# The down projection of both gated MLPs by seven block products per pair of output tiles

## The chip, the cores and the metric

The kernel runs on one NeuronCore of one Trainium2 chip. The metric is the device time of one execution in microseconds (us). All matrix work is float32, carried out as sums of three float32r products.

## What is computed

A trunk of two residual layers over 512 tokens of width 1024 and a final RMSNorm. Layer 0 mixes tokens by an S5 group and an mLSTM group, layer 1 by sliding-window attention. Each layer ends with the gated MLP that this change is about:

```python
def conv_gated_mlp(xn, w_up, conv_w, conv_b, w_down):
    gate, val = jnp.split(xn @ w_up, 2, axis=-1)
    return (jax.nn.silu(causal_dwconv(gate, conv_w, conv_b)) * val) @ w_down

h = h + conv_gated_mlp(rmsnorm(h, norm_ffn_g[layer]), ffn_w_up[layer], ffn_conv_w[layer],
                       ffn_conv_b[layer], ffn_w_down[layer])
```

`w_up` is 1024 x 5632, `w_down` is 2816 x 1024. The hidden width 2816 is 22 blocks of 128.

## The kernel before

Everything is held transposed: features on the 128 partitions, the 512 tokens along the free axis. `h` is the residual stream (8 blocks). A float32 product is made exact enough by splitting both operands into a float32r high part and the rest: `whi` and `wlo` for a weight tile, `ahi` and `alo` for an activation. `block3` then issues three matmuls per 128 x 128 block (high x high, high x low, low x high), each over 512 tokens. ScalarE (ACT) makes the high parts with a copy, VectorE (DVE) the low parts with a subtraction (`split_hi`, `split_lo`); weight tiles (512 KB) come by DMA into two buffers of `raw` and go on to a ring of four in `whi` and `wlo`. The load of a tile waits until `split_lo` of the tile two ahead of it is done.

**Up projection.** The first 4 of the 22 hidden blocks (`PLAIN`) go that way. The other 18 go in pairs, a gate tile with its value tile, by the seven-product form of a 2 x 2 block product: class `Pair`, 18 per layer. The activations are cut in quarters (4 blocks x 256 tokens): `b11`, `b21`, `b22` and the differences `t1` to `t4`. The weights of a pair are cut in quarters too and combined. GpSimd (POOL) makes the sums s1 and s3 in `fold` and three low parts (`pair_s1`, `pair_s3`, `pair_gate_lo`, `pair_keep_lo`, `pair_s3_lo`), DVE makes s2 and s4 in PSUM and three low parts (`pair_s2`, `pair_s2_lo`, `pair_s4`, `pair_s1_lo`, `pair_s4_lo`), ACT the high parts. TensorE (PE) then runs seven products P1, P2, P6, P5, P7, P3, P4 in that order, `quarter`, each 12 matmuls over 256 tokens, and DVE adds them up in `pair_u2`, `pair_u4` and `pair_row`. Convolution and gate (`pair_tap`, `pair_conv`, `pair_silu`, `pair_gated`) follow and write block j of the activation `a32`. The quarters of the activations are made once per layer, before pair 0: `turned_x` on POOL (the differences), `x_high` on ACT, `x_low` on DVE.

**Down projection.** For each of the 8 output tiles m, three weight tiles (8, 7 and 7 blocks) and 22 calls of `block3`. The four PSUM banks 0 to 3 take turns, so that a tile may start while three others wait to be added to `h`:

```python
            def down(i, m):
                pe.wait_ge(out_freed, i * 4 + (O_DN[l] + m - 3))
                for part, ks in enumerate(parts):
                    t = T_DN[l] + 3 * m + part
                    pe.wait_ge(lo_done, i * 12 + (t + 1))
                    for k in ks:
                        if k in ready:
                            pe.wait_ge(*ready[k])
                        ins = block3(bank[(O_DN[l] + m) % 4][:, :], t % RING, k - ks[0], ahi[:, k, :],
                                     alo[:, k, :], k == 0, k == FJ - 1)
```

The first tile takes each block k as it becomes ready, the last ones (`a_low`) while it already runs. Each engine works its list in the order in which it is written; semaphores with counts tie the lists together. An instruction that waits holds up all behind it on its engine.

Of the kernel before, what the change touches and what calls it, by code (L numbers as in the profile page):

```python
# [48 lines left out]
T_UP = [27, 77]  # L49
T_DN = [T_UP[0] + 2 * PLAIN, T_UP[1] + 2 * PLAIN]  # L50
T_QKV = T_DN[0] + 3 * KB
NQKV = 10
T_WO = T_QKV + NQKV
T_END = T_DN[1] + 3 * KB
# [11 lines left out]
NPAIR = FJ - PLAIN  # L66
# [4 lines left out]
A_GROUPS = ((2, 6), (6, 10), (10, 14), (14, 18), (18, 20), (20, 21), (21, 22))  # L71
A_POOL = ((2, 4),)
A_DVE = ((4, 6), (6, 8), (8, 10), (10, 12), (12, 14), (14, 16), (16, 18), (18, 20), (20, 21), (21, 22))
X_HI = {"b11": 1, "b21": 2, "t1": 3, "t3": 4, "t2": 5, "b22": 7, "t4": 8}
A_FIRST_HI, HI_EACH, LO_EACH, TURNED_EACH = 6, 8 + len(A_GROUPS), 7 + len(A_DVE), 5 + len(A_POOL)


def a_group(j):
    return 9 + [k for k, (j0, j1) in enumerate(A_GROUPS) if j0 <= j < j1][0]
# [41 lines left out]
class Pair:  # L121
# [12 lines left out]
    def block(self):  # L134
        return PLAIN + self.c

# [36 lines left out]
def build(nc, wstream, spairs, xT, params, bc, consts, band, outT, u_scratch):  # L173
# [78 lines left out]
    alo_at = base + size([P, FJ, SEQ]) + 4 * LINE  # L252
    assert past_a + 2112 + 2 * 2048 + 1024 <= alo_at
    alo = at("alo", [P, FJ, SEQ], alo_at, f32r)
    a32 = at("a32", [P, FJ, SEQ], alo_at)
    raw2 = at("raw2", [P, 2, 8 * P], alo_at + size([P, FJ, SEQ]))
# [154 lines left out]
    p1_kept, keep_high, keep_low = half_in[0:3]  # L411
# [3 lines left out]
    rstd_bank = bank[6]  # L415

# [6 lines left out]
    last_bank = (bank[(O_DN[1] + KB - 1) % 4], bank[4])  # L423
# [16 lines left out]
    def _(sp):  # L440
# [71 lines left out]
        def pair_loads(l):  # L512
# [20 lines left out]
        loads(T_DN[0] + 1, T_QKV + 5)  # L533
        sp.wait_ge(tile_used, used_count(T_DN[0] + 3 * KB - 1))
# [18 lines left out]
    def _(pool):  # L553
# [2123 lines left out]
```

## Time and profile before

| what | value |
|---|---|
| median of 3 runs | 1029.65 us (1029.28 to 1033.05) |
| the profiled execution | 1028.86 us, its span 1027.3 us |
| TensorE busy | 1012.5 us, 99% of the span |
| VectorE, ScalarE, GpSimd busy | 68%, 53%, 48% |
| up pairs, layer 0 and layer 1 | about 256 to 426 us and 728 to 897 us |
| down projection, layer 0 and layer 1 | about 426 to 547 us and 897 to 1019 us |

The span is cut in stages that follow each other. A share over the whole says little: in the stretch of the up pairs DVE and POOL are near 80% busy, in that of the down projection under 50% and 10%.

### The profile page before, as it was taken

How to read it: one execution, taken by the hardware profiler on the slowest of the kernel's cores; microseconds unless marked ns; L12 is line 12 of the kernel's file. 1: busy time of each engine (PE TensorE's matmuls, PEld its weight loads, DVE VectorE, ACT ScalarE, POOL GpSimd, SP SyncE). 2: the span in 40 equal slices, each digit the busy share in tenths (PEclk: the TensorE clock that was granted, in tenths of full speed). 3: DMA queues.
4: the chain of work that ended last, by engine and by line, in shares of the span. 5: the costliest groups of instructions: out<-in, count | busy, mean ns of one | idle time of the engine just before them, and what ended most of it. 6: DMA issues, size and time to landing. Idle time of an engine off the chain costs nothing.

```text
span 1027.3 us, 18159 instructions
## 1 busy us (share of the span) xinstructions
PE 1012.5 (99%) x6848; PEld 886.4 (86%) x6848; DVE 700.5 (68%) x1020; ACT 541.0 (53%) x939; POOL 489.4 (48%) x437
## 2 busy tenths in 40 slices
PE   9999999999999999999999999999999999999997
PEld 8787778887999999978888777888999999978886
DVE  6798774499877787853334776568987787873332
ACT  6545674456665666732323565464666666732221
POOL 8998930454878777200110122244877877501100
PEclk9999999999999999999999999999999999999999
DMA  7442024221333232243224111242223223133322
GB/s 240 164 122 53 26 96 173 94 103 62 124 123 123 87 118 82 82 144 123 102 100 156 51 54 63 66 140 83 94 112 123 108 97 123 61 125 121 103 82 82
DMA packets 31293, 107.47 MB, mean 105 GB/s; under 512 B 7232, under 2 KB 9536, under 8 KB 26368
## 3 DMA queue, kind: packets, MB, share of 16 engines
q1 hardware_dynamic: 31232, 106.69, 30.5%
q8 instruction: 34, 0.56, 0.2%
q14 instruction: 27, 0.22, 0.1%
HBM read 102.09 MB, written 3.15 MB: 102 GB/s over the span
## 4 chain that ended last, share of the span: by engine, by line
PE 81%; DVE 11%; issue 2%; ACT 2%; DMA 2%; SPq 1%; POOL 0%; DVEq 0%; ACTq 0%
PE bank L2054 15%; PE bank L2056 14%; PE bank L2055 14%; PE bank L2364 11%; PE bank L2363 11%; PE bank L2365 11%; DVE wlo L1379 2%; PE bank L2078 2%; DVE alo L1731 2%; DMA raw<-wstream 1%; DVE t_lo L1731 1%; PE bank L2503 1%; PE bank L2480 1%; DVE b_lo L1731 1%; DVE a L1801 1%
## 5 line engine op out<-in xcount | busy, mean ns | idle before, releaser
L1379 DVE TENSOR_TENSOR wlo<-raw,whi 128x1024 fp32r<-128x1024 f32 x105 | 143.7, 1373 | 104.2 <-ACT whi L877 103.7
L877 ACT ACTIVATE whi<-raw 128x1024 fp32r<-128x1024 f32 x105 | 110.7, 1055 | 141.5 <-PE bank L2056 87.4
L2363 PE MATMUL bank<-t_hi,shi 128*128 128x256 f32 x576 | 159.9, 278 | 3.6 <-DVE bank L1737 3.6
L2365 PE MATMUL bank<-t_hi,slo 128*128 128x256 f32 x576 | 159.7, 277 | 0.0
L2364 PE MATMUL bank<-t_lo,shi 128*128 128x256 f32 x576 | 159.7, 277 | 0.0
L2054 PE MATMUL bank<-xhi,whi 128*128 128x512 f32 x384 | 151.9, 396 | 0.8 <-DVE wlo L1379 0.8
L2055 PE MATMUL bank<-xlo,whi 128*128 128x512 f32 x384 | 149.6, 390 | 0.0
L2056 PE MATMUL bank<-xhi,wlo 128*128 128x512 f32 x384 | 149.6, 390 | 0.0
L2054 PE MATMUL bank<-ahi,whi 128*128 128x512 f32 (+1 forms) x374 | 141.5, 378 | 0.5 <-DVE alo L1731 0.3
L2056 PE MATMUL bank<-ahi,wlo 128*128 128x512 f32 (+1 forms) x374 | 140.9, 377 | 0.0
L2055 PE MATMUL bank<-alo,whi 128*128 128x512 f32 (+1 forms) x374 | 140.9, 377 | 0.0
L583 POOL TENSOR_TENSOR ssum<-ssum,sq 128x512 f32<-128x512 f32 x27 | 39.5, 1464 | 201.1 <-ACT sq L883 201.1
L802 POOL TENSOR_TENSOR slo<-raw,shi 128x1024 fp32r<-128x1024 f32 x36 | 88.8, 2468 | 82.0 <-ACT shi L1179 82.0
L2363 PE MATMUL bank<-b_hi,shi 128*128 128x256 f32 x432 | 119.5, 277 | 0.0
L2364 PE MATMUL bank<-b_lo,shi 128*128 128x256 f32 x432 | 119.3, 276 | 0.0
L2365 PE MATMUL bank<-b_hi,slo 128*128 128x256 f32 x432 | 119.3, 276 | 0.0
L2363 PEld LDWEIGHTS bank<-t_hi,shi 128*128 128x128 f32 x576 | 108.7, 189 | 4.0 <-DVE bank L1737 4.0
L2365 PEld LDWEIGHTS bank<-t_hi,slo 128*128 128x128 f32 x576 | 108.9, 189 | 0.0
L2364 PEld LDWEIGHTS bank<-t_lo,shi 128*128 128x128 f32 x576 | 108.8, 189 | 0.0
L2054 PEld LDWEIGHTS bank<-xhi,whi 128*128 128x128 f32 x384 | 72.1, 188 | 17.6 <-DVE wlo L1379 1.2
L2056 PEld LDWEIGHTS bank<-xhi,wlo 128*128 128x128 f32 x384 | 72.1, 188 | 15.2
L2055 PEld LDWEIGHTS bank<-xlo,whi 128*128 128x128 f32 x384 | 72.1, 188 | 14.6 <-issue 0.2
(309 smaller groups left out, 2240.3 us busy)
## 6 DMA issues: line engine op xcount, KB each, us to landing
raw<-wstream SPq DMA_DIRECT2D x105, 512.0 KB, 3.3
raw<-spairs SPq DMA_DIRECT2D x36, 1024.0 KB, 4.8
xin<-xT SPq DMA_DIRECT2D x8, 256.0 KB, 6.3
raw<-wstream SPq DMA_DIRECT2D x8, 256.0 KB, 5.4
h<-xT SPq DMA_DIRECT2D x1, 2048.0 KB, 8.1
u_scratch<-uperm SPq DMA_DIRECT2D x1, 1024.0 KB, 5.4
uc<-u_scratch SPq DMA_DIRECT2D x8, 128.0 KB, 4.4
bandsb<-band SPq DMA_DIRECT2D x1, 1024.0 KB, 4.8
```

The costliest lines, as they stand in the source:

```text
L583: G.tensor_tensor(ssum[:, :], ssum[:, :], sq[:, m % 2, :], ALU.add).then_inc(acc_done, 1)
L802: G.tensor_tensor(slo[:, two, :], raws[p.par][:, 0, :].rearrange("p (b f) -> p b f", b=2), shi[:, two, :].bitcast(f32), ALU.subtract).then ...
L877: A(whi[:, t % RING, :], raw[:, t % RAWS, :], ACT.Copy).then_inc(hi_done, 1)
L1379: V.tensor_tensor(wlo[:, t % RING, :], raw[:, t % RAWS, :], whi[:, t % RING, :].bitcast(f32), ALU.subtract).then_inc(lo_done, 1)
L1731: V.tensor_tensor(dst, src, hi.bitcast(f32), ALU.subtract).then_inc(sem, 1)
L2054: MM(dst, wh, rhi, start=start, stop=False)
L2055: MM(dst, wh, rlo, start=False, stop=False)
L2056: return MM(dst, wl, rhi, start=False, stop=stop)
L2078: return nc.tensor.transpose(dst, src, ident[0:k, 0:k])
L2363: MM(dst, wh, hi[:, b, :], start=b == 0, stop=False)
L2364: MM(dst, wh, lo[:, b, :], start=False, stop=False)
L2365: ins = MM(dst, wl, hi[:, b, :], start=False, stop=b == 3)
```

## The change

Of the 22 blocks of the down projection, 0 to 5 (`KEPT`) stay plain: one weight tile of 6 blocks for each m, and two PSUM banks in turn (1 and 3) in place of four. Blocks 6 to 13 and 14 to 21 are two chunks. In each chunk the eight output tiles go as four pairs (m, m+1) through the same class `Pair` and the same engines' routines, so that a layer has 26 pairs: 18 up and 8 down, numbered 0 to 25 here. The quarters of the activations are now made three times per layer, for the up pairs and for each chunk, from `a32`. Each down pair ends with an addition of two rows of `h` (`pair_added`, two operands in SBUF, 128 x 1024), each plain tile with one (`kept_added`, one operand in PSUM, 128 x 512). The core of the diff (lines left out at "..."):

```diff
-NPAIR = FJ - PLAIN
+NUP = FJ - PLAIN
+CHUNKS, KEPT = 2, 6
+NPAIR = NUP + CHUNKS * KB // 2
...
+    def kept_bank(m):
+        return bank[(1, 3)[m % 2]][:, :]
...
             for q in range(2, NPAIR):
...
+                if q == NUP + 1:
+                    pair_used(Pair(l, NUP - 1))
+                    for t in range(T_DN[l], T_DN[l] + KB):
+                        load(t, t % RAWS, t - 1)
+                    sp.wait_ge(lo_done, T_DN[l] + KB)
+                else:
+                    pair_used(Pair(l, q - 2))
                 sp.dma_start(raws[q % 2][:, :, :], spairs[NPAIR * l + q]).then_inc(pair_in[q % 2], 16)
...
             pair_tap(last.before())
             pair_p1(last)
             a_high(l, 2, 6)
             pair_silu(last.before())
             act.wait_ge(product_done, last.count(7, P2))
-            split_hi(d0)
-            a_high(l, 6, 10)
...
+            split_hi(d0, w=KEPT * P)
+            x_high(l, "b11", product_done, last.count(7, P2), 0)
             act.wait_ge(product_done, last.count(7, P5))
+            split_hi(d0 + 1, w=KEPT * P)
             act.wait_ge(product_done, last.count(7, P3))
+            split_hi(d0 + 2, w=KEPT * P)
+            x_high(l, "b21", product_done, last.count(7, P3), 0)
             pair_tap(last)
+            split_hi(d0 + 3, w=KEPT * P)
             pair_silu(last)
...
+            x_high(l, "t4", xt_made, made + 9, 0)
+            split_hi(d0 + 6, w=KEPT * P)
+            pair_s1_copy(p)
+            split_hi(d0 + 7, w=KEPT * P)
+            pair_gate_hi(p)
...
+        def kept_added(l, m):
+            wait_tile_used(dve, T_DN[l] + m)
+            V.tensor_tensor(h[:, m, :], h[:, m, :], kept_bank(m), ALU.add).then_inc(out_freed, 1)
+
+        def pair_added(p):
+            m, made = p.rows(), parts_of(p)
...
+            both = drow_pair[:, :, 0:2 * QW]
+            V.tensor_tensor(h[:, m:m + 2, :], h[:, m:m + 2, :], both, ALU.add).then_inc(down_added, 1)
...
+            for q in range(NUP + 1, LAST):
+                p = Pair(l, q)
+                pair_row(p.before())
+                pair_added(p.before())
+                pair_s4_lo(p)
+                pair_s2(p.after())
+                pair_u2(p)
+                finished(p.before())
+                pair_s2_lo(p.after())
+                pair_s4(p.after())
+                pair_s1_lo(p.after())
+                if p.chunk() == 0:
+                    x_low(l, next(names), 1)
+                pair_u4(p)
+                if p.chunk() == 0:
+                    x_low(l, next(names), 1)
+                    if q == NUP + 3:
+                        x_low(l, next(names), 1)
...
+            finished(p.before())
+            split_lo(T_QKV)
+            pair_u4(p)
+            split_lo(T_QKV + 1)
+            split_lo(T_QKV + 2)
+            pair_row(p)
+            pair_added(p)
+            finished(p)
...
+            for m in range(KB):
+                t = T_DN[l] + m
+                pe.wait_ge(lo_done, t + 1)
+                if m == 1:
+                    pe.wait_ge(a_done, FJ * (l + 1))
+                if m >= 2:
+                    pe.wait_ge(out_freed, O_DN[l] + m - 1)
+                for k in range(KEPT):
...
+                    ins = block3(kept_bank(m), t % RING, k, ahi[:, k, :], alo[:, k, :], k == 0, k == KEPT - 1)
+                ins.then_inc(tile_used, 1)
+            for q in range(NUP, LAST):
+                pair(Pair(l, q))
```

`finished` makes, for the pairs of chunk 1, two low parts of the next layer's input (`xlo`, layer 0) or two rows of the output (`outb`, layer 1). The last pair of layer 1 runs its products as P1, P6, P5, P7, P3, P2, P4, so that the second half of the tokens is complete before the last two products. The sums of squares of `h` (`add_square`) for rows 0 to 3 move among the last two pairs on POOL.

How the lists change at the place where the plain tiles run, layer 0. First DVE before, from the sum `pair_u2` of the last up pair on (`wlo` is `split_lo` of a down tile, `alo` is `a_low`; `u4u` and the `rows` behind it are the last pair's sums, `bank<-rows,prm,bank` its convolution, `a<-rows,bank` its gate):

```order
L1768 TENSOR_TENSOR rows<-bank,p_68 128x2x256
L1801 TENSOR_TENSOR a_70<-rows,bank 128x512
L1379 TENSOR_TENSOR wlo<-raw,whi 128x1024
L1731 TENSOR_TENSOR alo<-a_70,ahi 128x1024 x2
L1773 TENSOR_TENSOR u4u_89<-bank,rows 128x512
L1776 TENSOR_TENSOR rows<-bank,u4u_89 128x256
L1731 TENSOR_TENSOR alo<-a_70,ahi 128x1024
L1379 TENSOR_TENSOR wlo<-raw,whi 128x1024
L1731 TENSOR_TENSOR alo<-a_70,ahi 128x1024
L1781 TENSOR_TENSOR rows<-bank,u4u_89 128x2x256
```

The same engine of the changed kernel, from the gate of the last up pair to the addition of the third plain tile (`h<-h,bank` is `kept_added`; `alo<-a,h_b` and `l_t<-f_t,h_t` are `x_low` of chunk 0):

```order
L1990 TENSOR_TENSOR a_70<-rows,bank 128x512
L1541 TENSOR_TENSOR wlo<-raw,whi 128x768
L1959 TENSOR_TENSOR h<-h,bank 128x512
L1541 TENSOR_TENSOR wlo<-raw,whi 128x768
L1893 TENSOR_TENSOR alo<-a_70,h_b_102 128x4x256
L1893 TENSOR_TENSOR alo<-a_70,h_b_103 128x4x256
L1959 TENSOR_TENSOR h<-h,bank 128x512
L1893 TENSOR_TENSOR l_t_105<-f_t_98,h_t_104 128x1024
L1541 TENSOR_TENSOR wlo<-raw,whi 128x768
L1893 TENSOR_TENSOR l_t_107<-f_t_100,h_t_106 128x1024
L1959 TENSOR_TENSOR h<-h,bank 128x512
```

What moved: six `alo` operations are gone, seven `x_low` have come, and the additions that free a bank for PE now stand behind two or three operations that read both operands from SBUF.

POOL of the changed kernel at the same place (before, one `alo` subtraction of 128 x 1024 and then only the sums of squares stand here). The `f0` rows are the differences of chunk 0, the `f1` rows those of chunk 1, `fold` and `slo` the weights of pairs 18 (`raw2`) and 19 (`raw`):

```order
L879 TENSOR_TENSOR f0_t1_98<-a32_70 128x1024
L879 TENSOR_TENSOR f0_t3_100<-a32_70 128x1024
L879 TENSOR_TENSOR f0_t2_99<-a32_70,f0_t1_98 128x1024
L879 TENSOR_TENSOR f0_t4_101<-a32_70,f0_t2_99 128x1024
L852 TENSOR_TENSOR fold_67<-raw2_72 128x512
L858 TENSOR_TENSOR fold_67<-raw2_72 128x512
L879 TENSOR_TENSOR f1_t1_112<-a32_70 128x1024
L879 TENSOR_TENSOR f1_t3_114<-a32_70 128x1024
L879 TENSOR_TENSOR f1_t2_113<-a32_70,f1_t1_112 128x1024
L864 TENSOR_TENSOR slo_74<-raw2_72,shi_73 128x1024
```

POOL, idle in this stretch before, has ten operations in a row, all SBUF to SBUF.

DVE of the changed kernel in the period of one down pair of chunk 0 (pair 20, with `h<-h,drow` the addition of pair 19):

```order
L1970 TENSOR_TENSOR h<-h,drow 128x1024
L1893 TENSOR_TENSOR slo<-bank,shi 128x512
L1899 TENSOR_TENSOR bank<-bank,raw 128x512
L1937 TENSOR_TENSOR drow<-bank,p_68 128x2x256
L1893 TENSOR_TENSOR slo<-bank,shi 128x512
L1907 TENSOR_TENSOR bank<-raw,bank 128x512
L1893 TENSOR_TENSOR slo<-bank,shi 128x512
L1893 TENSOR_TENSOR l_t_119<-f_t_112,h_t_118 128x1024
L1943 TENSOR_TENSOR du4u_92<-bank,drow 128x512
L1949 TENSOR_TENSOR drow<-bank,du4u_92 128x256
L1893 TENSOR_TENSOR l_t_121<-f_t_114,h_t_120 128x1024
L1955 TENSOR_TENSOR drow<-bank,du4u_92 128x2x256
```

Against an up pair, convolution and gate (three operations with one operand in PSUM) are gone; `h<-h,drow` and two `x_low`, with both operands in SBUF, have come.

## Rows read from the trace of the kernel before

**Rows 1.** The page, part 1: TensorE's busy time, share of the span, instructions.

```profile
PE 1012.5 (99%) x6848; PEld 886.4 (86%) x6848; DVE 700.5 (68%) x1020; ACT 541.0 (53%) x939; POOL 489.4 (48%) x437
```

**Rows 2.** Windows: busy us and instructions per engine, granted clock, DMA share, GB/s.

```profile
256.00:420.00 164.00, 162.81 (x1422) 162.84 (x1423) 131.19 (x207) 103.03 (x172) 126.37 (x84) 0.99 0.31 109
440.00:560.00 120.00, 120.00 (x530) 99.06 (x529) 49.91 (x53) 39.36 (x46) 9.69 (x8) 1.00 0.36 120
```

**Rows 3.** Timeline of PE, plain tiles and up pairs: start, duration, operation.

```profile
300.06 0.28 PE L2363 MATMUL bank<-b_hi,shi 128*128 128x256 f32 x1
...
301.08 0.28 PE L2363 MATMUL bank<-t_hi,shi 128*128 128x256 f32 x1
...
559.73 0.39 PE L2054 MATMUL bank<-xhi,whi 128*128 128x512 f32 x1
...
563.58 0.39 PE L2056 MATMUL bank<-xhi,wlo 128*128 128x512 f32 x1
```

**Rows 4.** Timeline of DVE and of POOL, 225 to 234 us.

```profile
225.84 1.42 DVE L1379 TENSOR_TENSOR wlo<-raw,whi 128x1024 fp32r<-128x1024 f32 x1
227.18 3.41 DVE L1379 TENSOR_TENSOR wlo<-raw,whi 128x1024 fp32r<-128x1024 f32 x1
230.51 3.43 DVE L1731 TENSOR_TENSOR b_lo<-xn,b_hi 128x1024 fp32r<-128x1024 f32 x1
...
226.13 3.38 POOL L817 TENSOR_TENSOR f_t<-xn,f_t 128x1024 f32<-128x1024 f32 x1
229.59 3.27 POOL L817 TENSOR_TENSOR f_t<-xn,f_t 128x1024 f32<-128x1024 f32 x1
```

**Rows 5.** Timeline of DVE and of POOL where the down tiles' splits begin.

```profile
422.16 1.92 DVE L1379 TENSOR_TENSOR wlo<-raw,whi 128x1024 fp32r<-128x1024 f32 x1
424.01 1.21 DVE L1731 TENSOR_TENSOR alo<-a,ahi 128x1024 fp32r<-128x1024 f32 x1
...
420.58 2.42 POOL L821 TENSOR_TENSOR alo<-a,ahi 128x1024 fp32r<-128x1024 f32 x1 [4.36 <-ACT ahi L1215]
```

**Rows 6.** Timeline of DVE and of POOL in the period of one up pair.

```profile
393.01 0.68 DVE L1801 TENSOR_TENSOR a<-rows,bank 128x512 f32<-128x512 f32 x1
...
392.24 2.42 POOL L802 TENSOR_TENSOR slo<-raw,shi 128x1024 fp32r<-128x1024 f32 x1 [2.06 <-ACT shi L1179]
394.62 1.30 POOL L807 TENSOR_TENSOR slo<-raw,shi 128x512 fp32r<-128x512 f32 x1
```

**Rows 7.** Timeline of DVE, the last up pair's work, and of ACT.

```profile
420.96 0.69 DVE L1768 TENSOR_TENSOR rows<-bank,p 128x512 f32<-128x512 f32 x1 [0.99 <-PE bank L2365]
...
426.28 0.68 DVE L1773 TENSOR_TENSOR u4u<-bank,rows 128x512 f32<-128x512 f32 x1
...
428.46 1.22 DVE L1379 TENSOR_TENSOR wlo<-raw,whi 128x1024 fp32r<-128x1024 f32 x1
...
433.60 0.75 DVE L1790 SCALAR_TENSOR_TENSOR bank<-rows,prm,bank 128x512 f32<-128x512 f32 x1
...
433.19 1.06 ACT L877 ACTIVATE whi<-raw 128x1024 fp32r<-128x1024 f32 x1 [0.95 <-DMA raw<-wstream]
```

**Rows 8.** Windows and timeline of PE: two waits of PE before early pairs.

```profile
258.00:260.00 2.00, 2.00 (x13) 2.00 (x12) 2.00 (x4) 1.60 (x3) 2.00 (x2) 0.58 0.31 49
...
257.19 0.36 PE L2363 MATMUL bank<-t_hi,shi 128*128 128x256 f32 x1 [2.37 <-DVE bank L1737]
```

**Rows 9.** Timeline of ACT and DVE at the end of layer 0.

```profile
550.09 0.61 ACT L901 ACTIVATE sum_hi<-ssum 128x512 fp32r<-128x512 f32 x1
...
549.40 1.14 DVE L1911 SCALAR_TENSOR_TENSOR xlo<-h,prm,xhi  x1 [1.62 <-ACT xhi L1309]
...
551.60 0.68 DVE L1392 TENSOR_TENSOR sum_lo<-ssum,sum_hi 128x512 fp32r<-128x512 f32 x1
```

**Rows 10.** Timeline of DVE at the kernel's end.

```profile
1018.91 0.42 DVE L2020 TENSOR_TENSOR h<-h,bank 128x256 f32<-128x256 f32 x1 [2.78 <-PE bank L2056]
...
1021.93 2.22 DVE L2025 TENSOR_TENSOR outb<-outb,rstd 128x256 f32<-128x256 f32 x4
```

More of the change, by code:

```diff
@@ new lines, in chunk_high, with next_high @@
+            def chunk_high(name):
+                if name == "t4":
+                    act.wait_ge(product_done, Pair(l, NUP + 3).count(7, P1))
+                if name == "b22":
+                    act.wait_ge(xt_made, made + 11)
+                need = {"b11": 13, "b21": 13, "t1": 10, "t3": 11, "t2": 12, "b22": 12, "t4": 13}[name]
+                x_high(l, name, xt_made, made + need, 1)
+            m_last = KB if l == 0 else KB - 2
+            n = 2 + 2 * l
+            def next_high(p):
+                act.wait_ge(down_added, p.added())
+                for m in (p.rows(), p.rows() + 1):
+                    A(xhi[:, m, :], h[:, m, :], ACT.Copy, scale=col("g_mix1", m)).then_inc(xhi_done, 1)
@@ L1817, in mlp @@
             g = "g_ffn%d" % l
-            first, last = Pair(l, 0), Pair(l, NPAIR - 1)
+            first, last = Pair(l, 0), Pair(l, NUP - 1)
             plain = [Pair(l, k - PLAIN) for k in range(PLAIN)]
@@ L1867, in mlp @@
             pair_u4(first)
-            for q in range(1, NPAIR - 1):
+            for q in range(1, NUP - 1):
                 period(Pair(l, q))
+            p = last.after()
             pair_row(last.before())
@@ L1918, in mlp @@
[L1918 to L1928 removed]
+            split_lo(d0 + 3, w=KEPT * P)
@@ new lines, in mlp @@
+            kept_added(l, 0)
+            split_lo(d0 + 4, w=KEPT * P)
+            x_low(l, "b11", 0)
+            x_low(l, "b21", 0)
+            kept_added(l, 1)
+            x_low(l, "t1", 0)
+            split_lo(d0 + 5, w=KEPT * P)
+            x_low(l, "t3", 0)
+            kept_added(l, 2)
+            x_low(l, "t2", 0)
+            x_low(l, "b22", 0)
+            split_lo(d0 + 6, w=KEPT * P)
+            kept_added(l, 3)
+            x_low(l, "t4", 0)
+            pair_s2(p)
+            split_lo(d0 + 7, w=KEPT * P)
@@ new lines, in mlp @@
+            p = Pair(l, LAST)
+            pair_row(p.before())
+            pair_added(p.before())
+            pair_s4_lo(p)
+            if l == 1:
+                finished(p.before())
+                return
+            pair_u2(p)
+            finished(p.before())
+            split_lo(T_QKV)
+            pair_u4(p)
+            split_lo(T_QKV + 1)
[3 more added lines that the diff above has]
+            finished(p)
+            split_lo(T_QKV + 3)
```

571 lines of the change are left out of this document (353 added, 218 removed).

## The prediction

> **What bounds the kernel now.** I read the page's busy times first: TensorE (PE) is busy 99% of the span [rows 1], so a change pays by taking matmul time away, as long as nothing else becomes late. Then the windows by stage [rows 2]: DVE and POOL are 80% and 77% busy beside the up pairs, 42% and 8% beside the down projection, so the down projection has room in which vector work may hide. Then the timeline, for what one operation costs and what happens when DVE and POOL work together; the sum turns on that.
>
> **PE work removed.** Plain matmuls over 512 tokens start 3.85 us / 17 = 0.2265 us apart, the pairs' over 256 tokens 1.02 us / 9 = 0.1133 us apart [rows 3]. Before, a layer's down projection is 8 x 22 x 3 = 528 of the first: 119.6 us. Now it is 8 x 6 x 3 = 144 of them (32.6 us) and 8 x 7 x 12 = 672 of the second (76.1 us), 108.7 us. Saved: 10.9 us a layer, **21.8 us** in both.
>
> **What lies on DVE and POOL.** Two operations that both work from SBUF to SBUF don't overlap. At 225.84 DVE runs `wlo`; the POOL operation that starts at 226.13 takes 3.38 us where the same size takes 2.42 alone [rows 6], and DVE's next `wlo`, 1.2 us alone [rows 5, 7], takes 3.41, the one behind it 3.43 [rows 4]. Ends and starts fit a strict turn: DVE, POOL, DVE, POOL, DVE, each waiting for the other's whole operation. Likewise the 1.92 us at 422.16 end 1.1 us after POOL's at 420.58 does [rows 5]. Where one of DVE's operands is in PSUM it does not wait: 0.68 us under a 2.42 us POOL operation [rows 6]. The Trainium skill (GPSIMD Engine Reference, Specifications) says that GpSimd's SBUF interfaces are shared with VectorE, for instructions with two SBUF inputs and for those in a 2-port mode. By that page layer 1's `finished`, of one input, waits too, which no row shows; by rows of the first kind it doesn't, and the sum would differ by 1 or 2 us.
>
> The old down projection left POOL idle. The new one gives both engines such work all along. Per layer, with starts 1.13 us apart for 1024 columns and 0.6 us for 512 on DVE, 0.87 us between them for 768, and 2.36 and 1.26 us on POOL (the durations less the overlap of 0.05 us or so with the next) [rows 5 to 7]: DVE 8 splits 7.0, two `a_low` 2.3, 14 `x_low` 15.8, 8 additions 9.0, six low parts 4 (layer 0); POOL weights of 8 pairs at 2.36 + 4 x 1.26 = 7.4, so 59.2, 8 differences 18.9, two squares 2.5. Together 118.7 us, one after another, where PE needs 108.7 and they start 4.2 us ahead of it (422.2 against 426.4). So the port alone asks for about 5 us more than PE's work does, if it is never idle.
>
> **The plain stage, laid out.** I put the lists of front end to end, in trace time of layer 0, in strict turns. PE's tile is 18 x 0.2265 = 4.1 us; a tile's load takes 3.6 us from the low part that frees its buffer to the split (the low part of 428.46 ends at 429.6, the split starts at 433.19, released by the DMA) [rows 7]. DVE: `wlo` 0 and two `a_low` until 425.3, the last pair's u4 until 426.4; POOL starts t1 at 425.3, so `wlo` 1 runs 427.7 to 428.6, `pair_row` to 429.2, `wlo` 2 waits for t3 until 430.9, the convolution (0.66 + 0.79) ends 433.3, SiLU 433.9, gate 434.6. PE finished tile 0 at 430.5; tile 1 writes bank 3, the convolution's, and waits for that gate: **4.1 us**. `wlo` 3 waits for t4 (436.5), `wlo` 4 for s1 (438.7), `x_low` b11 for s3 (440.8), b21 for chunk 1's t1 (444.3); only then, 446.1, `kept_added` 1. Tile 3 needs its bank at 442.7: **3.3 us**. `x_low` t1 and `wlo` 5 wait for t3 and t2 of chunk 1, `kept_added` 2 ends 454.0, needed at 450.2: **3.8 us**. `wlo` 7 waits for the load behind `wlo` 5 and for POOL: **0.8 us** at tile 6. In all 12.0 us; the stage ends at 471, not 459. Without turns only the first wait stays, 2.3 us: ACT's SiLU stands behind the split of tile 3, whose load waits for `wlo` 1. Both layers: **+24.0**, lower bound +4.6.
>
> **The pairs, laid out.** A period of PE is 84 x 0.1133 = 9.52 us, each product 1.36 us. In periods 19 to 21 the port has POOL's 7.4, DVE's `pair_added` 1.13 and two or three `x_low` 2.3 to 3.4: 10.8 to 11.9 us. I count from the start of P1 of pair 18; ACT splits the next pair's gate quarters only when P2 is done (its slots), 2.7 us into a period, then POOL takes 2.4 for `gate_lo`, and P1 of the next pair can start 3.3 us before it must: that is the reserve. Pair 19 (from 9.5): `row` 10.1, addition behind `s3_lo` 12.2, then s1 and s3 of pair 20 until 14.7; `gate_lo` 17.2, `x_low` 19.6, u4 20.7, `x_low` 22.0, s1 23.3. Pair 20 (from 19.0): `row` 22.6, addition 24.4, s3 25.7, `gate_lo` 28.1 for P1 at 28.6; `x_low` 30.4 and 32.8, u4 31.5. Pair 21 (from 28.6): `row` 33.4, addition 35.2, `s4_lo` 35.8 where P3 wants it at 35.4; `gate_lo` 38.9; three `x_low` and u4 until 46.0. Pair 22 (from 39.0): `row` 46.6, s3 47.3, addition 48.4, `s4_lo` 49.0, wanted at 45.8. PE waits 0.5 + 0.4 + 3.2 us. Periods 22 on have no `x_low`, but in layer 0 7.4 + 1.1 + 1.3 for `finished`, and 2.5 more of squares near the end; at P1, P6 and P5 of the last pair PE waits 1.5 + 0.6 + 1.0 us more: **+7.2** in layer 0. Layer 1's `finished` is cheaper: **+5.8**. Lower bound zero: without turns DVE has 8.9 of 9.5 us.
>
> **End of layer 0.** PE took the next layer's first tile without a wait, the last low parts coming at 549.4 and the sum of squares at 551.6 [rows 9]. Now two rows of `h` come at once, and DVE's list has `split_lo` of tile T_QKV+2 ahead of the last `pair_row`. Its load can start only when T_QKV is split: +3.6, +1.0 high part, +1.1 low part, then row 0.7, addition 1.1, high parts 1.3, low parts 0.7 each. On time, PE waits 1.2 us for them and 2.9 for the mean; from the late pairs of the layout 5.9 and 3.7: **+9.6**, lower bound +4.1.
>
> **End of the kernel.** Before, 8.4 us lie between the last half's addition at 1018.91 [rows 10] and the end. Now a row sum stands ahead, the addition and square are of two rows, the mean has three matmuls in place of two, and the first half's factor too comes only after P4: **+2.0** (0.9 to 4).
>
> **Clock.** After the 2.37 us wait at 257.19 the granted clock was 0.58 for some 4 us [rows 8], 1.2 GHz in part. It would fall after waits of 3 to 4 us as well, but the slower tile ends while PE would be waiting for DVE anyway; only 0.8 us a layer comes through: **+1.6** (0 to 10).
>
> **Sum.** -21.8 + 24.0 + 13.0 + 9.6 + 2.0 + 1.6 = +28.4 on 1028.9 of the profiled execution, 1057.3; the median of the runs is 0.8 higher: **1058 us**. Not on the path: the loads (load bytes of the down tiles are the same 512 KB for 8 instead of 24 tiles, the pairs' 1 MB load has a whole period), and ACT, under 7 of 9.5 us.
>
> **Rivals.** *The turns don't delay what PE waits for (faster).* If an operation of POOL holds DVE only in part, or DVE gets ahead whenever it asks, what stays is 4.6 + 4.1 + 2.0: 1029.7 - 21.8 + 10.7 = **1018.6**. Rows 4 and 5 speak against it, the up pairs' calm for it only because their DVE work has PSUM operands. It decides once the waits of both layers are under 21.8 us, about 40% of my 50.
> *The port is shared in turns but well filled.* Then each layer ends some 5 us after PE's own work, at or before its earlier time: -21.8 + 9.6 + 4.1 + 2.0 gives **1023 to 1027**; halfway to my layout, 1035 to 1045. For it: my layout leaves the port idle for about a tenth of the time because lists wait for loads and for products; against it: the order is fixed, and `kept_added` stands behind three such operations.
> *The clock falls and stays low behind each wait*: 8 waits at up to 1.7 us: **1068**.
>
> **Chances.** My layout (1047 to 1068) 0.60, halfway 0.10, port well filled 0.10, turns without effect 0.15, clock on top 0.05. A measurement of this kernel tells about 0.5%, 5 us, from no change. Faster 0.24, same 0.08, slower 0.68. The likeliest one's own range is 1047 to 1068; with the cases of the other sign, of which the outermost is partly left out, 1019 to 1067.
>
> **What would show it.** PE idle at tiles 1, 3 and 4 of the plain stage, released by `a<-rows,bank` and `h<-h,bank`, DVE's `x_low` at 2 to 3.5 us each beside POOL, and the stretch from the last up pair to the first down pair at 40 to 45 us; P3 of pairs 21 and 22 released by `slo`; a down pair period over 9.52 us. If PE goes through the plain tiles in 33 to 36 us, the prediction is wrong, by the turns. Wrong otherwise: a third reader on the port, a slower period from matmul operands in new places, or a load that ACT waits for.

## The result and the profile after

| | before | after |
|---|---|---|
| median of 3 runs | 1029.65 us | **1053.6 us** (1052.01 to 1065.77) |
| ratio | | **1.023**, 95% interval 1.0171 to 1.0289 |
| the profiled execution, its span | 1028.86, 1027.3 us | 1053.6, 1051.8 us |
| granted TensorE clock, mean | 0.996 | 0.983 |

The changed kernel is slower by 24 us. The page of the changed kernel, part 1 (before: [rows 1]):

```profile
PE 1006.9 (96%) x7362; PEld 901.4 (86%) x7362; DVE 817.9 (78%) x1162; ACT 589.0 (56%) x1050; POOL 680.5 (65%) x530
```

The matmuls should have taken 21.8 us away and PE's busy time fell by 5.6 only, for the most part since some of them ran at a lower clock. DVE is busy for 117 us more, POOL for 191 us more; an operation that waits for the other engine counts as busy in these figures. The windows of the changed kernel (columns as in [rows 2]): plain tiles and down pairs of layer 0 and of layer 1, and the end of layer 0. In place of the calm down projection of [rows 2] DVE and POOL are as busy as beside the up pairs.

```profile
426.00:473.00 47.00, 38.88 (x153) 30.71 (x152) 37.78 (x33) 16.50 (x21) 30.32 (x13) 0.89 0.23 79
473.00:555.00 82.00, 78.88 (x673) 78.11 (x671) 71.98 (x86) 47.97 (x78) 74.45 (x42) 0.98 0.26 91
...
915.00:959.00 44.00, 35.88 (x152) 28.49 (x151) 37.52 (x32) 16.59 (x22) 30.61 (x13) 0.96 0.25 85
959.00:1041.00 82.00, 78.15 (x673) 76.79 (x672) 72.50 (x91) 43.57 (x72) 73.55 (x42) 1.00 0.22 78
562.00:577.00 15.00, 9.83 (x25) 7.33 (x26) 7.92 (x12) 7.49 (x10) 3.62 (x2) 0.55 0.43 140
```

In the plain stage PE is idle for 8.1 us of 47 and for 8.1 of 44, in the pairs for 3.1 and 3.9 of 82. What it waited for, over the whole span (total, times, longest):

```profile
PE bank L2305 <- DVE a L1990: 8.3, 2, 4.2
PE bank L2305 <- DVE h L1959: 7.9, 4, 3.1
PE bank L2615 <- DVE slo L1893: 5.1, 2, 2.5
PE bank L2305 <- DVE xlo L2109: 4.9, 1, 4.9
PE bank L2325 <- DVE sum_lo L1554: 2.6, 1, 2.6
PE bank L2615 <- DVE bank L1899: 2.4, 1, 2.4
```

The last of these stands in the kernel before too [rows 8]; the five above it, 28.8 us, are new. Where they lie in layer 0, in the timeline of PE:

```profile
435.07 0.47 PE L2305 MATMUL bank<-ahi,whi 128*128 128x512 f32 x1 [4.17 <-DVE a L1990]
...
445.98 0.47 PE L2305 MATMUL bank<-ahi,whi 128*128 128x512 f32 x1 [0.81 <-DVE h L1959]
...
453.49 0.77 PE L2305 MATMUL bank<-ahi,whi 128*128 128x512 f32 x1 [3.14 <-DVE h L1959]
...
520.95 0.58 PE L2615 MATMUL bank<-ahat,shi 128*128 128x256 f32 x1 [2.53 <-DVE slo L1893]
...
564.53 0.80 PE L2305 MATMUL bank<-xhi,whi 128*128 128x512 f32 x1 [4.87 <-DVE xlo L2109]
...
570.10 0.80 PE L2325 MATMUL bank<-sum_hi,mean_r 128*128 128x512 f32 x1 [2.64 <-DVE sum_lo L1554]
```

These are the first matmuls of plain tiles 1, 3 and 4, P3 of pair 22, the next layer's first tile and its mean. What made them late stands in DVE's list. Its timeline in the plain stage, and POOL's:

```profile
426.75 2.33 DVE L1541 TENSOR_TENSOR wlo<-raw,whi 128x768 fp32r<-128x768 f32 x1
...
429.60 2.54 DVE L1541 TENSOR_TENSOR wlo<-raw,whi 128x768 fp32r<-128x768 f32 x1
...
434.24 0.69 DVE L1990 TENSOR_TENSOR a<-rows,bank 128x512 f32<-128x512 f32 x1 [0.65 <-ACT bank L1248]
434.85 2.84 DVE L1541 TENSOR_TENSOR wlo<-raw,whi 128x768 fp32r<-128x768 f32 x1
...
439.57 5.67 DVE L1893 TENSOR_TENSOR alo<-a,h_b 128x1024 fp32r<-128x1024 f32 x2
445.16 0.67 DVE L1959 TENSOR_TENSOR h<-h,bank 128x512 f32<-128x512 f32 x1
...
454.40 1.21 DVE L1893 TENSOR_TENSOR alo<-a,h_b 128x1024 fp32r<-128x1024 f32 x1
455.54 0.94 DVE L1541 TENSOR_TENSOR wlo<-raw,whi 128x768 fp32r<-128x768 f32 x1
```

```profile
425.85 5.47 POOL L879 TENSOR_TENSOR f_t<-a 128x1024 f32<-128x1024 f32 x2 [9.24 <-DVE alo L1893]
431.28 5.59 POOL L879 TENSOR_TENSOR f_t<-a,f_t 128x1024 f32<-128x1024 f32 x2
...
440.76 6.72 POOL L879 TENSOR_TENSOR f_t<-a 128x1024 f32<-128x1024 f32 x2
```

The same `wlo` of 128 x 768 takes 0.94 us when POOL is idle (455.54) and 2.33 to 2.84 us beside it in the rows shown (1.43 and 3.12 us in two others); two `x_low` take 5.67 us, one alone 1.21. The addition with its operand in PSUM takes 0.67 us wherever it stands: it doesn't wait itself, but what stands ahead of it does, so it starts at 445.16 and frees its bank at 445.8.

The stages of both traces, from first matmul to first matmul (the pairs of layer 1 to the end of the span):

| stage | before | after | difference |
|---|---|---|---|
| up to the down projection of layer 0 | 426.2 | 426.6 | +0.4 |
| down projection, layer 0 | 120.6 | 46.3 plain + 82.4 pairs | +8.1 |
| next layer's first tile to its first up pair | 176.6 | 188.3 | +11.7 |
| up pairs, layer 1 | 173.0 | 171.6 | -1.4 |
| down projection, layer 1, to the end | 130.9 | 43.5 + 81.7 + 11.4 | +5.7 |
| sum | 1027.3 | 1051.8 | +24.5 |

### The profile page after: what moved, and what is told of

Its sections match the earlier page's. It is cut to its first block and busy times, and to the rows that moved or that the text cites. A ratio compares the mean times of both kernels' runs of the same rounds, so it can differ in the third digit from the quotient of the medians.

```text
span 1051.8 us, 19517 instructions
## 1 busy us (share of the span) xinstructions
PE 1006.9 (96%) x7362; PEld 901.4 (86%) x7362; DVE 817.9 (78%) x1162; ACT 589.0 (56%) x1050; POOL 680.5 (65%) x530
## 5 line engine op out<-in xcount | busy, mean ns | idle before, releaser
L864 POOL TENSOR_TENSOR slo<-raw,shi 128x1024 fp32r<-128x1024 f32 x52 | 129.8, 2495 | 105.1 <-ACT shi L1271 105.1
L1541 DVE TENSOR_TENSOR wlo<-raw,whi 128x1024 fp32r<-128x1024 f32 (+1 forms) x73 | 111.0, 1525 | 25.8 <-ACT whi L969 25.7
L969 ACT ACTIVATE whi<-raw 128x1024 fp32r<-128x1024 f32 (+1 forms) x73 | 73.3, 1007 | 97.6 <-DMA raw<-wstream 62.8
L1893 DVE TENSOR_TENSOR slo<-bank,shi 128x512 fp32r<-128x512 f32 x156 | 106.4, 682 | 3.7 <-ACT shi L1277 2.2
L2305 PEld LDWEIGHTS bank<-xhi,whi 128*128 128x128 f32 x384 | 72.9, 190 | 24.5 <-DVE xlo L2109 5.3
L852 POOL TENSOR_TENSOR fold<-raw 128x512 f32<-128x512 f32 x52 | 76.6, 1473 | 11.2 <-DMA raw<-spairs 11.2
L874 POOL TENSOR_TENSOR slo<-fold,shi 128x512 fp32r<-128x512 f32 x52 | 75.7, 1456 | 11.0 <-ACT shi L1286 11.0
L2615 PEld LDWEIGHTS bank<-b_hi,shi 128*128 128x128 f32 x432 | 81.1, 188 | 0.5 <-DVE gpad L1882 0.5
```

What stands on the lines that cost most here:

```text
L852: G.tensor_tensor(fold[:, 0, :], raws[p.par][:, 1, 4 * P:], raws[p.par][:, 1, 0:4 * P], ALU.add).then_inc(pool_weights, 1)
L864: G.tensor_tensor(slo[:, two, :], raws[p.par][:, 0, :].rearrange("p (b f) -> p b f", b=2), shi[:, two, :].bitcast(f32), ALU.subtract).then ...
L874: G.tensor_tensor(slo[:, p.slot(P7), :], fold[:, 1, :], shi[:, p.slot(P7), :].bitcast(f32), ALU.subtract).then_inc(pool_weights, 1)
L969: A(whi[:, t % RING, 0:w], raw[:, t % RAWS, 0:w], ACT.Copy).then_inc(hi_done, 1)
L1541: V.tensor_tensor(wlo[:, t % RING, 0:w], raw[:, t % RAWS, 0:w], whi[:, t % RING, 0:w].bitcast(f32), ALU.subtract).then_inc(lo_done, 1)
L1893: V.tensor_tensor(dst, src, hi.bitcast(f32), ALU.subtract).then_inc(sem, 1)
```

## The experiments

The looped up pairs run at one of two paces from one execution to the next, some 6 us apart per layer (last section), whatever the kernel, so that medians of the kernel before lay between 1029.65 and 1034.96 us in the four sets of runs. I therefore compare the lengths of the stages that were changed, in the profiled executions, and give the ratio to the kernel before on the same chip beside them. A stage that an experiment leaves as it was still moves by 1 to 3 us with the clock (the plain stages of experiments 4 and 7). "Exit" is the third stage of the table. The pairs of layer 0 reach to the next layer's first matmul, those of layer 1 to their own last one.

| kernel | plain, layers 0 and 1 | pairs | exit | median, ratio to before (95%) |
|---|---|---|---|---|
| the change | 46.3, 43.5 | 82.4, 81.7 | 188.3 | 1053.6, 1.023 |
| 1 narrow differences | 36.2, 37.6 | 80.2, 80.1 | 187.5 | 1038.16, 1.0032 (0.999 to 1.0074) |
| 2 additions sooner | 39.5, 39.5 | 82.4, 82.2 | 188.5 | 1045.98, 1.0121 (1.0078 to 1.0165) |
| 3 three banks | 40.7, 40.3 | 81.8, 81.7 | 188.3 | 1049.47, 1.014 (1.0066 to 1.0213) |
| 4 last rows first | 45.0, 43.5 | 81.8, 81.7 | 184.2 | 1050.09, 1.0125 (1.0041 to 1.0209) |
| 5 before, busy GpSimd | 128.4 and 138.7 for 120.6 and 130.9 | | 176.6 | 1051.12, 1.0163 (1.0115 to 1.0212) |
| 6 all, differences on VectorE | 36.0, 35.4 | 84.5, 83.0 | 184.0 | 1039.1, 1.0049 (1.0017 to 1.0081) |
| 7 one low part later | 43.4, 45.1 | 82.9, 82.8 | 187.8 | 1057.7, 1.0257 (1.0213 to 1.0302) |
| 8 experiments 2 to 4 together | 39.4, 39.5 | 82.5, 82.5 | 184.1 | 1045.56, 1.0135 (1.0084 to 1.0186) |
| 9 as 6, with 7 undone | 34.4, 34.4 | 82.5, 82.3 | 184.1 | 1032.41, 1.0008 (0.9973 to 1.0043) |
| 10 as 9, differences narrow | 33.1, 33.0 | 80.3, 80.1 | 184.1 | 1028.55, 0.9977 (0.9944 to 1.0009) |

The theory: POOL and DVE take turns, operation by operation, wherever both work from SBUF to SBUF; the waits of PE come from that and from the order of DVE's list. The rival: the turns don't matter, and the waits come from the order and the banks alone.

**1. POOL's work in the plain stage is made small**, at the same places in the lists. ScalarE spreads the narrow differences to full width, so the output is no longer the reference's.

```diff
-            G.tensor_tensor(xf[c, name], xf[c, a], xf[c, b], ALU.subtract).then_inc(xt_made, 1)
+            w = QW if c < 0 else THIN
+            G.tensor_tensor(xf[c, name][:, :, 0:w], xf[c, a][:, :, 0:w], xf[c, b][:, :, 0:w],
+                            ALU.subtract).then_inc(xt_made, 1)
...
```

> The changed kernel, but GpSimd's 14 differences for the chunks (seven us-long 128 x 1024 operations per layer in the plain stage, one later) are computed over 32 of 256 columns and spread from there by ScalarE; the low parts of t1 to t4 are taken from the high parts twice. The values of these quarters are wrong, every other engine has as many operations of the same size as before. Theory of turns (VectorE's operations with two SBUF operands wait for GpSimd's whole operation): VectorE's x_low and split rows beside them fall from 2.3 to 2.8 us to about 1.0 to 1.5, additions to h come in time, the waits at plain tiles 3 and 4 go, the one at tile 1 falls from 4.2 to about 2.3 us, the plain stage falls from 46 to 36 us in each layer, the time from 1053.6 to 1030 to 1035 us. Rival, the lists' order and the loads alone make VectorE late: waits at tiles 1, 3 and 4 as before, time within 3 us of 1053.

DVE's timeline, at the same operations as above, and the windows of the plain stage and the pairs:

```profile
432.70 0.95 DVE L1552 TENSOR_TENSOR wlo<-raw,whi 128x768 fp32r<-128x768 f32 x1
433.57 0.68 DVE L1971 TENSOR_TENSOR h<-h,bank 128x512 f32<-128x512 f32 x1
...
435.14 2.62 DVE L1904 TENSOR_TENSOR alo<-a,h_b 128x1024 fp32r<-128x1024 f32 x2
```

```profile
425.70:461.90 36.20, 33.33 (x147) 27.06 (x147) 26.44 (x31) 16.30 (x21) 13.05 (x12) 1.00 0.31 102
461.90:541.00 79.10, 76.88 (x673) 76.34 (x671) 70.67 (x86) 47.67 (x78) 72.07 (x41) 1.00 0.27 94
```

DVE's list is the same, and its operations are back near their own length (2.62 us for the two `x_low` that took 5.67). PE's waits at tiles 3 and 4 are gone, that at tile 1 is 2.87 us in place of 4.17, and the clock is 1.00 in this layer. The plain stages are 10.1 and 5.9 us shorter, the clock's share included. The median, 1038.2 us, is above the 1030 to 1035 of the expectation, but far from the rival's 1053. This rules out the rival. The differences are also ready sooner here, which could make `x_low` early by itself; `wlo` reads none of them and shortens as well.

**2. The additions stand sooner in DVE's list**. The expectation says each behind one operation; in the edit those of tiles 1 to 3 stand behind two operations from SBUF to SBUF in place of three (`kept_added` 1, for example, behind `wlo` and `x_low` b11, ahead of b21).

> The changed kernel with the additions of plain tiles 1 to 4 moved ahead in VectorE's list, each behind one operation with two SBUF operands in place of two or three; nothing else. Theory of turns with late additions: the waits at tiles 3 and 4 (0.8 and 3.1 us) and the lower clock that follows fall away, the one at tile 1 (4.2 us) stays; 4 to 6 us a layer, about 1043 us. Rival, the port's total is what counts (well filled, the order is no matter): the waits come back elsewhere before the first down pair, time within 3 us of 1053.

The waits for `h` fell from 7.9 us to under 1, the wait for the gate stayed at 4.0: 39.5 us in place of 46.3 and 43.5. The median is 1046.0 us for about 1043 expected. So turns alone don't stop PE; they do where an operation that PE waits for stands behind several that take turns.

**3. Three banks in place of two.**

```diff
-        return bank[(1, 3)[m % 2]][:, :]
+        return bank[(7, 1, 3)[m % 3]][:, :]
...
-                if m == 1:
+                if m == 0:
+                    pe.wait_ge(p1_kept, Pair(l, NUP - 1).count(1, 1))
+                if m == 2:
                     pe.wait_ge(a_done, FJ * (l + 1))
-                if m >= 2:
-                    pe.wait_ge(out_freed, O_DN[l] + m - 1)
+                if m >= 3:
+                    pe.wait_ge(out_freed, O_DN[l] + m - 2)
...
+            pe.wait_ge(out_freed, O_DN[l] + KB - 1)
```

> The changed kernel with three PSUM banks (7, 1, 3) for the plain tiles in place of two, the convolution's bank first used by tile 2; the lists of all other engines are the same. Theory: tile 1 no longer waits for the last up pair's gate (4.2 us gone), later tiles wait for additions that come when they came before, but with one more tile in hand; the plain stage falls from 46 to about 39 us, the time to about 1040 us. Rival, PE's waits only mirror the port, whose work ends when it ends: under 3 us gained per layer, 1048 or more.

The gate's wait went from 4.17 to 0.92 us, and the waits for the additions moved and grew: 10.8 us in all in place of 7.9, still 3.13 at the longest. The stage is 5.6 and 3.2 us shorter, 40.7 and 40.3 us where the theory said 39, and the median of 1049.5 us is nearer to the rival's 1048 or more than to the theory's 1040. A bank more helps with one late operation, not with a list that is late.

**4. The last rows of `h` come ahead of the split of tile T_QKV+2** on ACT and DVE.

> The changed kernel with the split of the third tile of layer 1's first projection moved behind the last row sum, addition and low parts of layer 0, on ScalarE and VectorE. Theory (the load of that tile holds the last rows up): the 4.9 us wait for xlo and the 2.6 us for sum_lo fall to about 1 and 2 us, 4 us in all, 1049 to 1050 us; the rest of the trace as before. Rival, the rows are late for the pairs' sake: unchanged.

The wait for `xlo` fell from 4.87 to 1.25 us, that for the mean rose from 2.64 to 4.21, since what follows ends when the sum of squares does. The exit is 4.1 us shorter.

**5. The kernel before, with 24 additions of 128 x 512 on POOL** at the start of each down projection.

```diff
...
+            for k in range(24):
+                G.tensor_tensor(fold[:, 1, :], fold[:, 0, :], fold[:, 0, :], ALU.add).then_inc(spun, 1)
+                pool.wait_ge(spun, SEEN + 24 * l + k + 1)
```

> The kernel before, with 24 additions of 128 x 512 within fold on GpSimd behind its last work for each down projection, each waiting for the one ahead; nothing reads them. Theory of turns: VectorE's splits of the down tiles (two SBUF operands, 1.23 us alone) that fall among them take 1.3 to 2.6 us, GpSimd's own additions up to 2.5 in place of 1.3, the additions to h (one PSUM operand) stay at 0.69; PE has 3 us of reserve there, so the time stays within 5 us of before. Rival, the two share the memory by parts or not at all: splits at 1.23 to 1.4.

DVE's timeline and POOL's:

```profile
439.06 2.06 DVE L1736 TENSOR_TENSOR alo<-a,ahi 128x1024 fp32r<-128x1024 f32 x1
...
454.95 4.04 DVE L1384 TENSOR_TENSOR wlo<-raw,whi 128x1024 fp32r<-128x1024 f32 x2
```

```profile
429.87 41.87 POOL L854 TENSOR_TENSOR fold<-fold 128x512 f32<-128x512 f32 x24
...
459.96 1.04 POOL L854 TENSOR_TENSOR fold<-fold 128x512 f32<-128x512 f32 x1
```

Most of the `wlo` and `alo` took 1.7 to 2.06 us where they take 1.22 [rows 7], and POOL's additions started 1.74 us apart on average, where one with DVE idle beside it takes 1.04 us (459.96); the gate and the other operations with one operand in PSUM kept theirs. That the time would stay was wrong: in both layers together PE waited 5.8 us for `wlo` and 3.3 for `alo`, and with slower matmuls behind these waits each layer lost 7.8 us. The calm of the kernel before rests on POOL's idleness, nothing else of the change being in it.

**6. All of it together**: experiments 2 to 4 and 7, and the three differences of chunk 1 on DVE, behind the plain tiles, in place of POOL.

```diff
-            turned_x(l, "t1", "b12", "b11", a_done, FJ * (l + 1), 1)
...
+        def diff_x(l, name, a, b, sem, need):
+            dve.wait_ge(sem, need)
+            V.tensor_tensor(xf[1, name], xf[1, a], xf[1, b], ALU.subtract).then_inc(xt_made, 1)
```

> The changed kernel with the sooner additions, the three banks, the last rows first, one x_low moved from the period of pair 21 to that of pair 22, and three of the four differences for the second chunk made by VectorE (1.13 us each) where it waits for plain tiles, in place of GpSimd (2.36 us each). Theory of turns: the plain stage 35 us (33 for PE alone), pair 22's P3 waits under 1 us, 1026 to 1031 us. Rival, PE is held by something that the layout doesn't have: plain stage over 39 us.

The plain stage came down to 36.0 and 35.4 us, the pairs rose to 84.5 and 83.0, and the median of 1039.1 us missed the 1026 to 1031 expected. PE waits 4.7 us for `l_t`, in two (the part that was moved in experiment 7), and 2.6 and 2.2 us at P1 of pair 18 for an addition in bank 7. This last wait still lies in the plain stage; behind it, in layer 0, the pairs began at the lower clock:

```profile
467.00:470.00 3.00, 3.00 (x15) 3.00 (x15) 3.00 (x3) 0.39 (x1) 1.48 (x2) 0.50 0.18 22
```

**7. One of the three low parts of pair 21 moves into the next period**, ahead of pair 22's work.

```diff
+                if q == NUP + 4:
+                    x_low(l, next(names), 1)
...
-                    if q == NUP + 3:
-                        x_low(l, next(names), 1)
```

> The changed kernel with the last of chunk 1's seven x_low moved from the period of pair 21, which had three, to that of pair 22. Theory: P3 of pair 22 waits 2.5 us because that period asks 11.9 us of the port; with 10.8 the wait falls to 0.5 to 1.5 us and the lower clock behind it goes, 2 to 4 us over both layers, 1050 us. Rival, the port's backlog of the periods before makes the wait: unchanged.

PE's timeline at that place (0.34 and 2.36 us in place of 2.53):

```profile
513.42 0.39 PE L2615 MATMUL bank<-ahat,shi 128*128 128x256 f32 x1 [0.34 <-DVE slo L1893]
...
517.46 0.36 PE L2615 MATMUL bank<-h_t,shi 128*128 128x256 f32 x1 [2.36 <-DVE l_t L1893]
```

The expected 2 to 4 us did not come. P3 has its weights now, and P4, the next product, waits for the part that was moved: the wait changed its name and kept its size. The rival of the expectation held: here the place of one operation only moved the wait along.

**8. Experiments 2 to 4 together.**

> The changed kernel with the sooner additions, the three banks and the last rows first together, all work as before on its engines. By the layout in turns: tile 2 waits under 1 us for the gate, the additions come in time, plain stage 35 to 37 us in each layer in place of 46.3 and 43.5, the exit of layer 0 4 us less, 1030 to 1034 us. Rival, the port is the bound and the stage can't fall under its own sum: 39 us or more, as each of the three alone left it (39.5, 40.7).

The plain stage, 39.4 us, is no shorter than with experiment 2 alone, and the median is 1045.6 us for 1030 to 1034 by the layout. The gate's wait is gone, and PE waits for what was late behind it:

```profile
PE bank L2304 <- DVE wlo L1540: 6.5, 4, 2.6
...
PE bank L2304 <- DVE h L1958: 2.9, 2, 1.5
```

The rival's number, 39 us or more, held. Its reason did so in part: DVE goes without a pause of even 0.1 us from 440.6 to 471.6, but POOL is idle for 7 us of them:

```profile
469.47 1.29 POOL L874 TENSOR_TENSOR slo<-fold,shi 128x512 fp32r<-128x512 f32 x1 [7.15 <-ACT shi L1286]
```

So it is not the port that is full but DVE's list, lengthened by its waits for POOL. What helps is fewer such waits: experiments 6 and 9 take three operations of 2.36 us from POOL and give DVE three of 1.13 us, and experiment 10 makes all eight small.

**9. As 6, but with 7 undone and the last plain tiles on banks 1 and 3.**

> As the kernel with all rearrangements and chunk 1's differences on VectorE, but without the later low part (the three low parts of pair 21 are back in its own period, since the move made two products wait 2.4 us each) and with the last plain tiles on banks 1 and 3, so that P1 of pair 18 finds its bank free after the fourth plain tile (it waited 2.6 us for the addition of the seventh). By the theory that the waits are made by what stands ahead in VectorE's list while it takes turns with GpSimd: both waits go, 2.6 us and some clock in each layer, the plain stage stays at 35 to 36 us up to the first down pair, the down pairs go from 84 to 80 to 82 us, and a profiled execution with both up projections at the quicker pace ends at 1026 to 1031 us: equal to the kernel before within 0.5%. By the rival that the pairs are long through the load on the port itself and not through the place of one low part, they stay at 83 us or more, the wait is found at another product, and the span ends above 1033 us at the quicker pace.

The windows of the plain stage and of the pairs, layer 0, and DVE's timeline in the plain stage, where POOL is idle between 438.4 and 447.3:

```profile
424.00:458.40 34.40, 33.56 (x147) 26.93 (x146) 33.68 (x31) 16.29 (x21) 19.76 (x10) 1.00 0.32 108
458.00:541.00 83.00, 80.50 (x676) 79.70 (x674) 75.59 (x91) 48.48 (x79) 77.47 (x42) 0.98 0.25 90
```

```profile
442.55 1.21 DVE L1889 TENSOR_TENSOR l_t<-f_t,h_t 128x1024 fp32r<-128x1024 f32 x1
```

PE is busy 33.56 of 34.4 us at full clock. The 2.6 us wait at P1 of pair 18 is gone, but P3 of pair 22 waits again, 2.31 and 2.54 us, as in the changed kernel. The pairs, 82.5 and 82.3 us, lie between the 80 to 82 of the theory and the 83 or more of the rival. The span was 1025.1 us with both up projections at the quicker pace, and over 12 runs the kernel equals the one before. Four rearrangements of the same arithmetic gave back the 2.3%.

**10. As 9, with the differences of both chunks narrow.**

> As the one above, and the differences of both chunks are made of 32 of their 256 columns only (the output is then not the reference's): the operations stay where they are, 0.1 to 0.4 us each in place of 1.1 to 2.4. It shows what all rearrangements leave for the seven-product form if its differences cost the port next to nothing. By the turns: plain stage 33 to 35 us, pairs 79 to 80 us, exit of layer 0 184 us as before, so at the quicker pace a span of 1020 to 1025 us, 0.3 to 0.8% under the kernel before: the most that this form can give here as long as the exit and the kernel's end stay as they are. By the rival that the matmul time saved is lost elsewhere than on the port, the span stays above 1028 us.

Plain 33.1 and 33.0 us for 32.6 of matmuls, pairs 80.3 and 80.1. The median is 4.7 us under that of the kernel before, the interval of the ratio takes in 1. The profiled execution had both up projections at the slower pace (span 1032.0 us); the two quickest of the 12 runs had spans of 1019.7 and 1020.9 us, the low end of the 1020 to 1025 expected at the quicker pace. Without its differences' cost on the port this form saves 120.6 - 113.4 = 7.2 us in layer 0's down projection, and loses 184.1 - 176.6 = 7.5 behind it: PE waits 4.2 us for the mean and 1.3 for `xlo`, and the clock takes the rest. What is left is layer 1's, 130.9 - (33.0 + 80.1 + 11.8) = 6.0 us.

## Why the prediction held, and where its terms were off

The time came out at 1053.6 us for 1058 predicted, by the likeliest case and its steps, though not with the sizes of all of its terms.

*The turns.* The layout had the gate end at 434.6 (trace: 434.9), `kept_added` 1 at 446.1 (445.8), `kept_added` 2 at 454.0 (453.3), the start of the pairs at 471 (472.9). The waits named for tiles 1 and 4 are there. The Trainium skill (SBUF — State Buffer, section "SBUF: two separate sides") calls the port pair that VectorE and GpSimd share an exclusive lock, held for a whole instruction; the rows agree (2.33 to 2.84 us for 0.94, and POOL's own 2.42 us operation at 3.36). Experiments 1 and 5, which take POOL's work away and add it with next to nothing else, show that the turns are the cause.

*Plain stage, +24.0 with 1.6 of clock for both.* Measured beyond 32.6 us of matmuls: 13.7 and 10.9 us, together 24.6 for 25.6. The parts were off: 8.1 us of waits a layer for my 12.0, and 5.6 and 2.8 us of slower matmuls for my 0.8. So the waits were priced 7.8 us too high and the clock 6.8 us too low; that their sum came out is luck. Tile 3's wait was 0.8 us and not 3.3: behind the first wait the matmuls of tile 1 ran slower, so that tile 3 came later to its bank. The windows show the clock behind the wait of tile 1, then behind that of tile 4 in layer 0 and in layer 1:

```profile
435.00:440.00 5.00, 4.92 (x15) 3.90 (x16) 5.00 (x4) 3.85 (x5) 5.00 (x3) 0.66 0.26 79
454.00:458.00 4.00, 4.00 (x11) 3.07 (x10) 4.00 (x5) 0.84 (x1) 0.00 (x0) 0.50 0.06 25
942.00:946.00 4.00, 3.91 (x17) 3.27 (x18) 4.00 (x5) 0.84 (x1) 0.00 (x0) 1.00 0.18 73
```

That waits and clock would overlap was said; which of them keeps the time was not right. Tile 6 did not wait. The waits of both layers are alike (4.17, 0.8 and 3.1 us), yet behind the third the clock fell in layer 0 only: this is why 46.3 us stand beside 43.5. In the same way PE waits some 2.4 us early in the up pairs of layer 0 in all twelve traces [rows 8]; the clock fell behind it in seven of them and stayed at full speed in five. What decides it no run here tells.

*Pairs, +7.2 and +5.8.* Beyond 76.1 us: 6.3 and 5.6. P3 of pair 22 was 2.53 us for 3.2. P3 of pair 21 and P1 of pair 22 did not wait, nor P1, P6 and P5 of the last pair of layer 0; 0.83 us came at the tile behind it. So the waits were over-sized, and matmuls that took longer than their pitch filled the rest: PE was busy 78.88 us in layer 0, part of it at the lower clock, and 78.15 us in layer 1 at a granted clock of 1.00.

*What was left out.* The old down projections took 120.6 us and, up to the last addition, 122.5 (896.4 to 1018.9), not the 119.6 of their matmuls at their pitch. The saving of 10.9 us was thus 1.0 us too small in layer 0 and 2 to 3 in layer 1; this is why the sum is about 4 us too high, the other terms being off by 1 to 2 us in both directions.

*Exit of layer 0, +9.6.* Measured 11.7, with the two waits at 4.87 and 2.64 us for 5.9 and 3.7. The step on the list was right; the term lacked the clock behind it. Of the 4.2 us beyond the waits the windows show the cause:

```profile
565.00:568.00 3.00, 2.46 (x6) 1.35 (x5) 1.36 (x2) 1.28 (x2) 2.86 (x2) 0.50 0.73 279
568.00:571.00 3.00, 0.90 (x2) 0.81 (x3) 0.69 (x1) 1.91 (x2) 0.66 (x1) 0.50 0.60 188
571.00:574.00 3.00, 3.00 (x8) 2.33 (x8) 1.17 (x4) 2.26 (x3) 0.00 (x0) 0.50 0.00 0
```

The clock is at 1.2 GHz (0.50) for the whole of 562 to 574, with two waits close together. My 0.8 us a layer was read from the one short wait of [rows 8]; that was the weakest step of the sum.

*Kernel's end, +2.0.* From the last addition to the end 10.6 us, for 8.4 before [rows 10]: +2.2.

*The rivals.* "Turns don't delay" fell with the trace and with experiment 1. "The port well filled" was not this kernel, but it is roughly experiment 9: I gave it 1023 to 1027, and the profiled execution, with the quicker pace in both layers, took 1026.9 us (the median of the 12 runs, 1032.4 us, is above the range). It took another order, a third bank and three operations less on POOL to reach it, as the argument against the rival said (the order is fixed, and `kept_added` stands behind three such operations). "The clock stays low" was partly so, and is inside the terms above.

## What to carry to other kernels

Before work is put on GpSimd beside VectorE, sum up the operations of both that work from SBUF to SBUF and lay them one behind the other: their sum is a lower bound of its own, here 119 us by the estimate of the prediction for 109 us of matmuls. It is not the time: the changed kernel took 46.3 + 82.4 = 128.7 us in layer 0, since lists in a fixed order leave one engine idle while the other waits. What TensorE waits for (an addition that frees a bank, a gate) should stand ahead of such operations in the list, not behind three; but order and banks give only what isn't load, and the rest has to be taken off the port. Price a wait of TensorE together with the slower matmuls behind it, from a stretch of the same kernel in which a wait of that size occurs, and price it as a range: equal waits did and did not cost clock here.

## What the runs showed that I had not expected

**An operation of one SBUF input takes turns too.** DVE's timeline near the end of the changed kernel, and POOL's:

```profile
1035.14 1.90 DVE L2116 TENSOR_SCALAR outb<-h,prm 128x512 f32<-128x512 f32 x2
```

```profile
1035.36 2.82 POOL L645 TENSOR_TENSOR ssum<-ssum,sq 128x512 f32<-128x512 f32 x2 [1.96 <-ACT sq L975]
```

Taken singly the two are 0.47 and 1.51 us; the four such operations of the two pairs before took 1.90 us for each first one and 1.51 for each second. The same operation in the kernel before, with POOL idle, took 0.49:

```profile
1002.94 0.49 DVE L1896 TENSOR_SCALAR outb<-h,prm 128x512 f32<-128x512 f32 x1
```

The first of the two started ahead of POOL's, the second ended at 1037.0, just after POOL's first of 1.40 us (to 1036.8). The prediction said that no row showed this. The Trainium skill (GPSIMD Engine Reference, Specifications) names instructions in a 2-port mode beside those with two SBUF inputs, and these rows would fit it; that this operation is in such a mode no row shows.

**The looped up pairs have two paces at the same granted clock.** The windows 280 to 400 and 760 to 880 us lie inside the loops. Experiment 9's:

```profile
280.00:400.00 120.00, 120.00 (x1061) 120.00 (x1060) 95.07 (x151) 75.58 (x127) 93.11 (x64) 1.00 0.32 114
```

Experiment 10's, whose up pairs are the same instructions:

```profile
280.00:400.00 120.00, 120.00 (x1021) 120.00 (x1021) 92.44 (x147) 72.44 (x121) 90.66 (x62) 1.00 0.29 105
```

PE is busy all the time at clock 1.00 in both, with 1061 or 1021 matmuls in 120 us: 0.1131 or 0.1175 us apart. No value between was seen in any of these windows, each layer of an execution falls to one or the other by itself, and over a layer's 16 looped pairs of 84 matmuls it makes 5.9 us. The kernel before and after had the quicker pace in both layers. What sets it no run here tells; two layers of it are about the 12 us over which the runs of one kernel spread, and it is why stages were compared.
